# Loading the memory tokens by column quarters and working the first left half chunk by chunk for both token tiles

## What is computed

```
mem_n = rmsnorm(mem, mem_norm)          # mem: 256 x 2048
k = mem_n @ wk[layer]                   # 2048 x 2048, both layers
v = mem_n @ wv[layer]
```

## Time and profile before

| | us |
|---|---|
| median of 3 runs | 2854.95 (2854.28 to 2855.2) |
| the profiled execution's own time | 2855.41 |
| its span, first to last instruction | 2853.7 |
| PE busy | 2836.3 (99%) |
| DVE busy | 2120.3 (74%) |
| ACT busy | 1546.7 (54%) |

### The profile page before, as it was taken

One profiled execution on the slowest core, in us unless ns is written; L12 is line 12 of the kernel. 1 busy time (PEld: TensorE's weight loads), 2 busy tenths in 40 slices (PEclk: granted clock), 3 DMA queues, 4 the chain that ended last, 5 costly groups with the idle time before them and its releaser, 6 DMA issues.

```text
span 2853.7 us, 31752 instructions
## 1 busy us (share of the span) xinstructions
PE 2836.3 (99%) x13038; PEld 2356.3 (83%) x13038; DVE 2120.3 (74%) x1454; ACT 1546.7 (54%) x1391; POOL 49.3 (2%) x102
## 2 busy tenths in 40 slices
PE   8999999999999999999999999999999999999998
PEld 7888888888888888888888888788888888888887
DVE  7888787669569988885456876669569888886444
ACT  6666555546346655664444765446446656655443
POOL 0000000000000000000000000000000000000000
PEclk9999999999999999999999999999999999999999
DMA  7674754655556546547555655655556566456552
GB/s 267 234 274 168 277 197 176 246 181 212 186 173 241 182 174 235 212 171 281 192 193 175 211 192 181 221 177 188 211 169 222 181 225 224 168 198 267 194 195 96
DMA packets 239233, 582.54 MB, mean 204 GB/s; under 512 B 8896, under 2 KB 8928, under 8 KB 223472
## 3 DMA queue, kind: packets, MB, share of 16 engines
q1 hardware_dynamic: 233792, 532.72, 52.6%
q0 software_dynamic: 4416, 37.29, 3.4%
q10 hardware_dynamic: 880, 10.49, 0.9%
HBM read 563.69 MB, written 16.78 MB: 203 GB/s over the span
## 4 chain that ended last, share of the span: by engine, by line
PE 97%; DMA 1%; DVE 1%; issue 1%; ACT 0%; SPq 0%; DVEq 0%; POOLq 0%; POOL 0%; ACTq 0%
PE ps L1842 95%; PE ps L1987 1%; PE ps L1973 1%; PE ps L2269 1%; DMA wide<-in_xattn_wk 0%; DMA memx<-in_mem 0%; ACT w_hi L585 0%; DVE w_lo L1143 0%; DVE w_lo L1137 0%; PE ps L2219 0%; ACT hx L691 0%; DVE act_lo L1282 0%; DVE hx L1354 0%; DVE xres L1829 0%; DVE hx L1343 0%
## 5 line engine op out<-in xcount | busy, mean ns | idle before, releaser
L1143 DVE TENSOR_TENSOR w_lo<-wide,w_hi 128x2048 fp32r<-128x2048 f32 x548 | 1244.4, 2289 | 449.5 <-ACT w_hi L585 446.3
L585 ACT ACTIVATE w_hi<-wide 128x2048 fp32r<-128x2048 f32 x548 | 1044.8, 1914 | 502.4 <-PE ps L1842 410.9
L1842 PE MATMUL ps<-w_hi,act_hi 128*128 128x512 f32 x3352 | 896.8, 391 | 0.2 <-ACT w_hi L598 0.2
L1842 PE MATMUL ps<-w_lo,act_hi 128*128 128x512 f32 x3352 | 891.2, 389 | 0.4 <-DVE w_lo L1143 0.4
L1842 PE MATMUL ps<-w_hi,act_lo 128*128 128x512 f32 x3352 | 891.4, 389 | 0.0
L1842 PEld LDWEIGHTS ps<-w_lo,act_hi 128*128 128x128 f32 x3352 | 629.2, 188 | 132.1 <-DVE w_lo L1143 1.2
L1842 PEld LDWEIGHTS ps<-w_hi,act_lo 128*128 128x128 f32 x3352 | 629.7, 188 | 131.4
L1842 PEld LDWEIGHTS ps<-w_hi,act_hi 128*128 128x128 f32 x3352 | 626.9, 188 | 130.8 <-issue 2.0
L1147 DVE TENSOR_TENSOR wide<-wide,wide 128x2048 f32<-128x2048 f32 x102 | 233.5, 2290 | 4.7
L1098 ACT ACTIVATE act_hi<-mid 128x256 fp32r<-128x256 f32 x80 | 33.5, 418 | 243.0 <-PE ps L1842 243.0
L585 ACT ACTIVATE w_hi<-w_sum 128x2048 fp32r<-128x2048 f32 x34 | 65.3, 1921 | 95.9 <-DVE w_sum L1147 88.5
(11 more groups left out here) (253 smaller groups left out, 1544.2 us busy)
## 6 DMA issues: line engine op xcount, KB each, us to landing
wide<-in_ffn_w_gate SPq DMA_DIRECT2D x88, 1024.0 KB, 8.0
wide<-in_ffn_w_up SPq DMA_DIRECT2D x88, 1024.0 KB, 7.3
wide<-in_ffn_w_down SPq DMA_DIRECT2D x88, 1024.0 KB, 4.8
wide<-in_odd_w_in SPq DMA_DIRECT2D x48, 1024.0 KB, 5.3
wide<-in_xattn_wk SPq DMA_DIRECT2D x32, 1024.0 KB, 7.6
wide<-in_xattn_wv SPq DMA_DIRECT2D x32, 1024.0 KB, 7.1
wide<-in_even_w_in SPq DMA_DIRECT2D x32, 1024.0 KB, 7.1
wide<-in_xattn_wq SPq DMA_DIRECT2D x32, 1024.0 KB, 5.1
```

The source lines that it names most:

```text
L585: nc.scalar.activation(w_hi[:, c % W_SLOTS, :], src, ACT.Copy).then_inc(hi_done, 2)
L1143: nc.vector.tensor_tensor(w_lo[:, c % W_SLOTS, :], src, w_hi[:, c % W_SLOTS, :].bitcast(F32), ALU.subtract).then_inc(lo_done, 2)
L1842: return nc.tensor.matmul(dst, lhs, rhs, start=start, stop=stop, skip_group_check=loose)
```

## The change

The memory comes by column quarters of both token tiles (512 KB each). Each is issued just before the chunk with the same rows. Chunk 0 is issued as two transfers of 512 KB, the first with a semaphore of its own. SP no longer waits for the memory. PE, ACT and DVE handle the memory quarter by quarter. Each quarter takes two banks, and one instruction of ACT and one of DVE covers 256 columns (both token tiles) where it covered 128. PE's new `opening_mem` multiplies a chunk for both token tiles before it goes to the next. It turns the quarter of the next chunk inside each chunk, behind 16 matmuls in chunk 0 and behind 8 in chunks 1 and 2. In all streams the order is now: quarter s, chunk s.

```diff
             def load(n, src):
-                if n == 1:
-                    for b in range(1, 4):
-                        memory(b)
-                    sp.wait_ge(mem_in[1], 16)
-                elif n < WIDE and n:
+                if 2 <= n < WIDE:
                     sp.wait_ge(wide_full[n - 2], 16)
-                if n == 3:
-                    sp.dma_start(memx[:, 1, :], mem[P:2 * P, :]).then_inc(mem_in[4], 16)
+                if n < 4:
+                    memory(n)
...
+                if n == 0:
+                    sp.dma_start(dst[:, 0:2, :], src[:, 0:2, :]).then_inc(first_half, 16)
+                    dst, src = dst[:, 2:4, :], src[:, 2:4, :]
                 sp.dma_start(dst, src).then_inc(wide_full[n % WIDE], 16)
...
-            round_mem(0, (0,))
-            split_halves(first, 0)
-            round_mem(0, (1, 2, 3))
-            for s in range(1, 4):
+            for s in range(4):
+                round_mem(s)
                 split_halves(first, s)
-            round_mem(1)
...
+            def transposed_mem(b):
+                pe.wait_ge(mem_in[b], 16)
+                for k in range(4):
+                    bank = WORK + 2 * (b % 2) + k // 2
+                    if k % 2 == 0:
+                        emptied(bank, plan["mem_norm"], b // 2)
+                    for m in range(MT):
+                        ins = nc.tensor.transpose(...)
+                    if k % 2:
+                        ins.then_inc(work_full[bank], 1)
+            def opening_mem(st):
...
+                for s in range(4):
+                    for ms in ((0, 1),) if s < 3 else ((0,), (1,)):
+                        for parts in (HI_HI, LO_HI, HI_LO):
+                            for k in range(4):
...
+                                        pe.wait_ge(hi_ev, hi_ev_at["mem_norm"] + 2 * s + k // 2 + 1)
+                                        pe.wait_ge(hi_done, 2 * (c + s) + k // 2 + 1)
...
+                                for m in ms:
+                                    last = part_of(4 * s + k, m, (c + s) % W_SLOTS, k, ps[:, m, :], parts)
+                            if s < 3 and parts is (HI_HI if s else LO_HI):
+                                transposed_mem(s + 1)
```

More of the change, by code:

```diff
@@ L273, in build @@
         x_again = sem("x_again")
-        mem_in = [sem(f"mem_in{b}") for b in range(4)] + [sem("mem_in_other")]
+        mem_in = [sem(f"mem_in{b}") for b in range(4)]
+        first_half = sem("first_half")
         pv_done = sem("pv_done")
@@ L404, in memory @@
                 cols = slice(b * NB, (b + 1) * NB)
-                sp.dma_start(memx[:, 0, cols], mem[0:P, cols]).then_inc(mem_in[b], 16)
+                sp.dma_start(memx[:, :, cols], mem.rearrange("(m p) n -> p m n", p=P)[:, :, cols])\
+                    .then_inc(mem_in[b], 16)
             sp.dma_start(vec_rows[16:32, :], mem_norm.rearrange("(k p) -> k p", p=P)).then_inc(small_in, 16)
-            memory(0)
             for l in range(LAYERS):
@@ L594, in split_halves @@
                 act.wait_ge(w_used, c + 1)
-                src = landed(st.n + s)
+                if c == 0:
+                    act.wait_ge(first_half, 16)
+                    src = wide[0][:]
+                else:
+                    src = landed(st.n + s)
                 for h in range(2):
+                    if c == 0 and h:
+                        landed(0)
                     part = slice(h * HALF, (h + 1) * HALF)
@@ L838, in round_tiles, with round_mem @@
                                                  ACT.Copy, scale=scale[:, t:t + 1]).then_inc(hi_ev, 1)
-            def round_mem(m, banks=range(4)):
+            def round_mem(b):
                 act.wait_ge(vec_done, 1)
[L845 to L850, removed]
+                for j in range(2):
+                    bank = WORK + 2 * (b % 2) + j
+                    act.wait_ge(work_full[bank], plan["mem_norm"]["rf"] + b // 2 + 1)
+                    for k in range(2):
+                        t = 4 * b + 2 * j + k
+                        ins = nc.scalar.activation(act_hi[:, t, :], ps[:, bank, k * T:(k + 1) * T], ACT.Copy,
+                                                   scale=vec[:, 16 + t:17 + t])
                     ins.then_inc(hi_ev, 1)
@@ L1491, in _, with rest_mem @@
             dve.sem_inc(bank_free[4], 1)
-            def rest_mem(m, banks=range(4)):
+            def rest_mem(b):
                 e0 = hi_ev_at["mem_norm"]
[L1496 to L1499, removed]
-                        ins = nc.vector.scalar_tensor_tensor(
[L1501 to L1507, removed]
+                for j in range(2):
+                    bank = WORK + 2 * (b % 2) + j
+                    dve.wait_ge(hi_ev, e0 + 2 * b + j + 1)
+                    for k in range(2):
+                        t = 4 * b + 2 * j + k
+                        ins = nc.vector.scalar_tensor_tensor(
+                            out=act_lo[:, t, :], in0=ps[:, bank, k * T:(k + 1) * T], scalar=vec[:, 16 + t:17 + t],
+                            in1=act_hi[:, t, :].bitcast(F32), op0=ALU.mult, op1=ALU.subtract)
+                    ins.then_inc(bank_free[bank], 1)
+            for s in range(4):
+                rest_mem(s)
                 split(first, s, (0, 1))
-            rest_mem(1)
             def x_roots():
@@ L2010, in transposed @@
                     if st.g is None:
-                        opening(name, source, turned_by[source])
+                        if source == "mem_norm":
+                            opening_mem(st)
+                        else:
+                            opening(name, source, turned_by[source])
                         quad(st, 1, turned(0))
@@ L2025, in output @@
                 quad_by_tile(second, 1, at_end=next_norm(nxt))
[L2027 to L2033, removed]
-                                                  memx[:, m, (4 * b + k) * P:(4 * b + k + 1) * P], ident[:])
-                    ins.then_inc(work_full[WORK + b], 1)
+            def transposed_mem(b):
[5 more added lines that the diff above has]
+                    for m in range(MT):
+                        ins = nc.tensor.transpose(ps[:, bank, (k % 2) * T + m * P:(k % 2) * T + (m + 1) * P],
+                                                  memx[:, m, (4 * b + k) * P:(4 * b + k + 1) * P], ident[:])
+                    if k % 2:
+                        ins.then_inc(work_full[bank], 1)
@@ new lines, in opening_mem @@
+            def opening_mem(st):
+                c, pl = st.c, plan["mem_norm"]
+                for m in range(MT):
+                    pe.wait_ge(bank_free[m], st.u + 1)
+                for s in range(4):
+                    for ms in ((0, 1),) if s < 3 else ((0,), (1,)):
+                        for parts in (HI_HI, LO_HI, HI_LO):
+                            for k in range(4):
+                                if ms[0] == 0 and k % 2 == 0:
+                                    if parts is HI_HI:
+                                        pe.wait_ge(hi_ev, hi_ev_at["mem_norm"] + 2 * s + k // 2 + 1)
+                                        pe.wait_ge(hi_done, 2 * (c + s) + k // 2 + 1)
+                                    elif parts is LO_HI:
+                                        pe.wait_ge(bank_free[WORK + 2 * (s % 2) + k // 2], pl["r"] + s // 2 + 2)
+                                    else:
+                                        pe.wait_ge(lo_done, 2 * (c + s) + k // 2 + 1)
+                                for m in ms:
+                                    last = part_of(4 * s + k, m, (c + s) % W_SLOTS, k, ps[:, m, :], parts)
+                            if s < 3 and parts is (HI_HI if s else LO_HI):
+                                transposed_mem(s + 1)
+                        if ms == (0,):
+                            last.then_inc(m0_done, 1)
+                    last.then_inc(w_used, 1)
@@ L2036, in _ @@
             turned_by = {pre: next_norm(pre) for pre in TURNS}
-            turned_by["mem_norm"] = transposed_mem
             turned_by["pre_mix0"] = transposes("pre_mix0", h_done, 0, y)
```

## The result

| 20 runs each | us |
|---|---|
| before | 2854.71 (2854.12 to 2857.5) |
| changed | 2859.48 (2856.85 to 2860.35) |
| ratio | 1.0014, 95% interval 1.0008 to 1.002 |
| the profiled execution, before and changed | 2855.41 and 2859.9; spans 2853.7 and 2858.2 |

The changed kernel is slower by 0.14% (0.08 to 0.2%), which is 4.0 us (2.3 to 5.7) between the means. The medians lie 4.8 us apart. I forecast a median of 2857.7, 2.8 above the 2854.95 of the three runs that I had; it came out at 2859.48, inside my own range of 2856 to 2859.8 by only 0.3. The times of the changed kernel stand in two groups with nothing between: 8 runs at 2856.85 to 2857.56 (middle 2857.2, +2.5 us) and 12 at 2859.28 to 2860.35 (middle 2859.7, +5.0).

The account below looks back on a forecast made before the run. PE bounds the kernel (2836.3 of 2853.7 us). Squares 3.2 us later, less 0.4 slack, delay the snapshot and fifth product by 2.8: 2854.95 + 2.8 = 2857.7 us; own range 2856 to 2859.8, 8 in 10 2854.2 to 2860.2.

Parts of the forecast that it names:

- The step that mattered: Behind 28 us, the start of the memory's squares matters more than PE's row; ACT's and DVE's row arrives 0.5 us later.
- Start of the strip: The strip's first matmul on PE comes at 9.3 us, 2.6 us before 11.93; bounds 8.9 to 10.0.
- rival of completions out of order: First half of chunk 0 lands late: first matmul at 10.0, 0.7 us more on ACT, 2858.4 us; chance 0.12.
- PE through the left half: PE's matmuls, transposes, slow pace and stalls end the left half at 37.45 us against 37.93, a gain of 0.5.
- the slow pace: PE runs slowly for 5.9 us from the first matmul: 14 matmuls, 2.7 us extra; bounds 1.4 and 4.0.
- rival A: PE's row governs, since slack in ACT's and DVE's row swallows the lateness before 73.33: 2854.5 us; chance 0.14.
- The squares: ACT's squares of the memory start at 31.65 us, 3.2 us later than before.
- The second half of the argument: Snapshot at 66.5, fifth product at 76.1 instead of 73.33; PE idles almost 3 us there, 1 before the last quarter's transposes.
- slack: On ACT, 0.23 us before the first snapshot and 0.2 in the copies to nat absorb 0.4 us of lateness.
- rival B: PE stays slow longer because of its early pauses; chunk 1 costs 4.8 us more: 2862.5 us; chance 0.06.
- S: The time of the strip's first matmul on PE: 9.3 us, bounds 8.9 to 10.0.
- The loads: Closing the traffic hole from SP's wait brings chunk 3 some 2 us earlier; valued at nothing, as PE reaches it about 32.

Follow-up runs that it names:

- first experiment: The changed kernel with ACT's two squares of the memory moved into its idle times inside the left half: 2854.64 us against 2854.43 before.
- third experiment: The kernel before with two extra 128x2048 squares (results unused) on ACT ahead of the memory's squares: 2858.53 us against 2854.43.
- the two late ones: The kernel before with extra unused squares on ACT ahead of the memory's squares: two of them 2858.53 us, one 2856.89 us.
- ninth: The eighth's kernel with ACT rounding one bank of a memory quarter and splitting its half chunk in turn: 2855.69 us against 2854.72 before.
- fifth experiment: The kernel before with one extra 128x2048 square (result unused) on ACT ahead of the memory's squares: 2856.89 us against 2854.94.
- fourth experiment: The kernel before with only SP's wait for the memory's quarter 1 taken out: 2853.72 us against 2854.43.
- second: The changed kernel with ACT's two squares of x moved into the idle time before the split of the first sum: 2855.62 us against 2854.43 before.
- twelfth experiment: The ninth's kernel with DVE's two scale computations of the memory moved into DVE's idle time before quarter 3: 2852.23 us against 2854.30 before.
- eighth: Changed kernel, memory's squares in left-half idle times, x's squares moved early, quarter 1 turned behind 8 matmuls of chunk 0: 2852.82 us against 2854.94 before.

## Why the prediction was right, and where it was short

- **What governs.** The step that mattered was that the start of the memory's squares counts more than PE's own row. The first and third experiments show it from both sides: take the lateness away with PE's order kept, and the loss is gone; add the lateness to the old kernel, and the loss is there in full.
- **Start of the strip.** Forecast 9.3, measured 9.79. The memory quarter let PE begin at 5.87 and not at 5.3. The first half of chunk 0 was not late: ACT went from rounding to it without a pause. The rival of completions out of order did not happen. The rows of before don't speak for it either: chunk 0 was seen at 8.86 and the memory quarters issued after it at 9.43, in the order of issue.
- **PE through the left half.** Forecast 37.45, measured 37.94. From the first matmul on that is 28.15 us, as forecast, but by terms that cancel, which is luck: the slow pace cost 3.0 us (16 matmuls in 6.7 us instead of 3.6) for 2.7, the 24 transposes 2.4 for 2.9 (8 take 0.79), and about 0.9 is left for PE's stalls (0.48 of it one wait before chunk 1) for 0.75. PE's gain on before was to be 0.5 by the sum. Against the true end of the half before, 38.15, the forecast was a gain of 0.7, and 0.2 came. This is not in the 2.8, since the wait for ACT decides there. It would have made rival A 0.2 us faster.
- **The squares.** Forecast 31.65, measured 31.98. They came 3.56 us late for 3.2 forecast, and up to the snapshot 0.64 of it was swallowed for 0.4. The two errors nearly cancel, 2.92 for 2.8, and that is luck as well.
- **The second half of the argument.** Forecast: snapshot at 66.5, fifth product at 76.1 with almost 3 us of idle time before it and 1 before the transposes. Measured: 66.65, 76.26, 1.96 and 1.53. Together that is 3.5 us for 3.8 forecast. The division was off, since `nat` was written at 65.0 and I had 64.3. That figure takes off all 0.4 us of slack, but 0.23 of it lies behind the copies to `nat`, at the snapshot. With 3.2 - 0.2 added to the end of the copies before (60.24 + 1.45) it would have been 64.7.
- **What was missing.** The sum had no term for what the idle time does to PE's clock. I had rival B lower the clock in chunk 1 and had not asked the same of the 3 us at 73. It cost 1.56 us in the profiled execution, of the 2.5 between the groups; without it the forecast of 2.8 stands against 2.5 in the lower group. My upper bound was made of S and the slow pace alone, so that the median with the fallen clock still lies within it is luck.
- **The loads.** Valued at nothing, and rightly so for this change. As an edit of its own in the old order it brings 0.7 us, since chunk 3 is waited for there.

Still open is why the groups lie 2.5 us apart in the changed kernel and 1.7 and 2.3 in the two late ones, and what decides whether the clock falls: the 1.95 us of the third experiment's profile and the 2.12 of the ninth's left it at 1.00. The rise of the clock at the start also differs between executions (16 matmuls took 5.61 us in the first experiment's profile and 6.68 in the changed kernel's), and the two may go together; I have no profile of the lower group to show it.

## What to carry to other kernels

When an edit lets the bound engine start earlier, look at what the engines behind it now do later. Work that sits behind the last paced step (here 3.8 us of squares) moves with it, and the wait shows 35 us downstream, at the first place where two rows of work meet. A wait of PE can cost more than its length, by what it does to PE's clock. Before reordering, fill the idle times: the two squares put into gaps of the new order gave back everything, and with the rest of the moves the kernel's median is 2.1 us below before, with 1 just inside the interval of the ratio.

## What the runs showed of the hardware

PE's granted clock fell after an idle time of only 2.0 us, in some executions of a kernel and not in others: with one such idle time in 5 of 11 runs (fifth experiment), in the changed kernel in 12 of 20, if the groups of times are read so. The 12 matmuls after it took 4.45 us at a granted clock of 0.62 (changed kernel), and 2.85 at 1.00 where it did not fall (third experiment). After idle times of 0.56 us (before, first and fourth experiment), 1.53 us (second) and even 2.12 us (ninth) no such groups show, so the length of the idle time alone doesn't decide it.

A GpSimd instruction on 128 elements that takes 0.55 us took up to 7.1 us while DVE ran two-operand instructions on SBUF without a break, and both took 1.08 us together when they began in an idle time of DVE (twelfth experiment). The Trainium skill (SBUF — State Buffer, section SBUF: two separate sides) says that the two engines share a pair of ports, held by one of them for a whole instruction while the other is blocked. The traces agree in part. The second power instruction took 2.4 us in the eighth and ninth experiments, about as long as one DVE instruction beside it (2.29). But the first one of the ninth took 7.1 us, while six DVE instructions passed, so the wait isn't always over after one. Why it wasn't there is open.
